# Gates of one dense tile scattered to memory as words, and 28 low parts of weights moved from GpSimd to VectorE

## Chip, cores and metric

One core of one Trainium2 chip. The metric is the device time of one execution in microseconds; lower is better. The kernel before took 2700.61 us (median of 3 runs, 2696.91 to 2716.93).

## What is computed

An encoder block: norm, a pooling and windowed-attention mixer with its output projection, norm, and an expert layer (PEER). The change touches the expert layer alone:

```python
def chunk(ht):                                   # 128 tokens
    q = (ht @ w_q).reshape(128, 8, 2, 128)       # 8 heads, 2 halves
    s = einsum('thpc,hpnc->thpn', q, subkeys)
    sv, si = top_k(s, 16)                        # 16 of 128 keys, each half
    cand_s = sv[:, :, 0, :, None] + sv[:, :, 1, None, :]
    cand_i = si[:, :, 0, :, None] * 128 + si[:, :, 1, None, :]
    top_s, top_pos = top_k(cand_s, 16)           # 16 experts a head
    expert = take_along_axis(cand_i, top_pos)
    gate = softmax(top_s)
    act = gelu(einsum('thkd,td->thk', u[expert], ht))
    return einsum('thkd->td', (gate * act) * v[expert])
```

There are 16384 experts (128 x 128), 1024 tokens of width 1024, so each token uses 8 x 16 = 128 gates.

## The kernel before

The 1024 tokens are 8 tiles of 128. Tiles 5 to 7 are "gathered": for each of their 128 gates a row of `u` and a row of `v` is fetched per token by an indirect DMA (GpSimd) and used on VectorE. Tiles 0 to 4 are "dense": every expert is computed for them on TensorE, and a full table of gates (zero where an expert isn't chosen) multiplies the result. Weights are multiplied in two parts, high and low: ScalarE rounds the raw piece `w_raw` to `w_hi` (`upper_ahead`, L961), and GpSimd makes `w_lo = w_raw - w_hi` (`lower_u`, L681). An item of the first dense stage is one 512 KB piece of `u` (or of the query weights, 16 of the 144 items) against 640 tokens: 48 matmuls of 320 columns (L1644), then Gelu (L955) and a store to `act_d` in HBM by SyncE.

The items fall into three stretches, which the text calls A, B and C:

- A, bodies 0 to 41 (2 items a body): the queries' items among them, while VectorE finds the best keys and pairs (`best_pairs`, `pair_keys`) and dots gathered `u` rows (`dot_row`, L1382). ScalarE takes the exponent of all gates at body 39; VectorE then divides by the sums (L1484 to L1486), and TensorE turns keys and gates (L1972) so that experts lie along partitions.
- B, bodies 42 to 61: 20 "strips" of 32 tokens. For four tokens at a time (`m`), VectorE writes one-hot tiles `is_i` and `gate_j` (L1508, L1512; ScalarE makes the fourth `gate_j`), TensorE multiplies them into a 128 x 128 gate table per token (`gates`, L1984, 4 times between the matmuls of each item), ScalarE copies it out (L989), and each strip of 2 MB goes to `g_d` in HBM. VectorE also dots 4 rows an item, GpSimd fetches 4 rows an item and makes one low part, which it starts after the item's first `gate_j` (a wait on `gj_done`).
- C, bodies 62 to 71: 20 items without gates. GpSimd makes one low part an item and fetches 3 or 4 rows, the last 40 of them `v` rows (L697), which VectorE adds with a scalar-tensor-tensor (`early_row`, L1397). ScalarE issues the first loads of stage 2 (`fetch`).

Each engine has its own program in a fixed order, and semaphores tie them. `w_raw`, `w_hi` and `w_lo` have two slots each: the load of a piece waits for the low part two items earlier, `w_hi` for TensorE's release of the slot, and TensorE waits for the low part. A row buffer is one of 8 (`RING`); in C the fetches run 6 rows ahead of the rows that VectorE has to have used by then.

Stage 2 reads `act_d` and the gates back (four dense tiles by `g_raw`, the fifth by `g_first`, 512 KB in runs of 1 KB), multiplies them (L1538, L1544), splits into high and low parts and multiplies with `v` (L2013), while GpSimd fetches the other `v` rows (L740) and VectorE adds them (L1588).

## Time and profile before

| quantity | us |
|---|---|
| median of 3 runs | 2700.61 |
| all runs | 2700.61, 2716.93, 2696.91 |
| profiled execution: span from first to last instruction | 2706.7 |
| TensorE busy (share of the span) | 2604.8 (96%) |
| VectorE busy | 2139.0 (79%) |
| GpSimd busy | 1490.1 (55%) |
| ScalarE busy | 881.3 (33%) |

The three runs have no record of what of them lies outside a span; the profiled execution's span is itself 6.1 us above the median of the three runs and inside their extent. A matmul's rows show pipelined instructions, so their distance in time is what one costs, not their length; an fp32 matmul appears as two rows.

### The profile page before, as it was taken

The numbers are of one execution on the slowest core, as the hardware profiler recorded it, in microseconds if no ns is written. First come the engines' busy times: TensorE is split into PE (matmuls) and PEld (weight loads), VectorE is DVE, ScalarE is ACT, GpSimd is POOL, SyncE is SP. The second block draws the span as 40 slices with busy tenths as digits, with TensorE's granted clock in tenths as the row PEclk, the third lists the DMA queues.
The fourth block names the chain that finished last, engine by engine and source line by source line (L and its number), as shares of the span: only waits on it lengthen the run. The fifth ranks groups of instructions, "written<-read, shape, count | busy, mean of one in ns | idle before, by whom it ended". The sixth has DMA issues, their size and how long they took to land.

```text
span 2706.7 us, 41554 instructions
## 1 busy us (share of the span) xinstructions
PE 2604.8 (96%) x15177; PEld 2334.8 (86%) x15177; DVE 2139.0 (79%) x4586; ACT 881.3 (33%) x1655; POOL 1490.1 (55%) x960
## 2 busy tenths in 40 slices
PE   7999989999999999989999999998999999999998
PEld 6777758999999999989999999986888787888887
DVE  6022273589888999999999995768998988998996
ACT  4223252222222222236666662222222222222222
POOL 1111020245666677766565557837777766776670
PEclk9999989999999999999999999998999999999999
DMA  4110013335777899989999999999999999999993
GB/s 147 47 32 24 24 56 125 107 108 164 278 273 257 306 317 318 338 307 354 389 373 377 379 394 348 406 341 366 388 388 388 353 384 370 386 385 388 384 382 128
DMA packets 296525, 763.31 MB, mean 282 GB/s; under 512 B 25808, under 2 KB 116304, under 8 KB 293584
## 3 DMA queue, kind: packets, MB, share of 16 engines
q0 software_dynamic: 110592, 402.70, 39.8%
q1 hardware_dynamic: 161280, 288.88, 30.8%
q10 hardware_dynamic: 24528, 70.26, 6.7%
q8 instruction: 54, 0.88, 0.1%
q14 instruction: 71, 0.58, 0.1%
HBM read 669.47 MB, written 92.27 MB: 281 GB/s over the span
## 4 chain that ended last, share of the span: by engine, by line
PE 63%; DVE 10%; DMA 6%; issue 4%; POOL 3%; ACT 1%; SPq 0%; DVEq 0%; ACTq 0%
PE bank L1644 27%; PE bank L2013 13%; PE wide L2013 10%; PE bank L1984 5%; DMA g_raw<-g_d 4%; PE bank L1893 3%; PE bank L1912 2%; DVE u_row L1382 1%; POOL w_lo L681 1%; DVE eq L1452 1%; DVE v_lo L1595 1%; POOL u_row L697 1%; PE bank L1921 1%; DMA u_row<-in_v,ids 1%; DVE route L1454 1%
## 5 line engine op out<-in xcount | busy, mean ns | idle before, releaser
L740 POOL DMA_INDIRECT d_row<-in_v,ids x344 | 591.7, 1720 | 276.6 <-DVE yg L1588 196.6
L1644 PE MATMUL bank<-h_hi,w_hi 128*128 128x320 f32 (+1 forms) x2368 | 562.3, 319 | 13.2 <-POOL w_lo L681 10.2
L1644 PE MATMUL bank<-h_hi,w_lo 128*128 128x320 f32 (+1 forms) x2368 | 545.7, 312 | 0.0
L1644 PE MATMUL bank<-h_lo,w_hi 128*128 128x320 f32 (+1 forms) x2368 | 544.9, 311 | 0.0
L681 POOL TENSOR_TENSOR w_lo<-w_raw,w_hi 128x1024 fp32r<-128x1024 f32 x144 | 358.4, 2489 | 289.2 <-ACT w_hi L961 158.1
L1382 DVE CUSTOM_DVE_ANT_0 u_row<-wide,u_row 128x1024 f32<-128x1024 f32 x384 | 449.1, 1219 | 18.0 <-DMA u_row<-in_u_rows,ids 15.8
L692 POOL DMA_INDIRECT u_row<-in_u_rows,ids x384 | 388.0, 1010 | 115.8 <-issue 74.1
L1588 DVE SCALAR_TENSOR_TENSOR yg<-d_row,uh,yg 128x1024 f32<-128x1024 f32 x344 | 426.0, 1276 | 1.4
L1644 PEld LDWEIGHTS bank<-h_hi,w_hi 128*128 128x128 f32 x2368 | 392.5, 189 | 19.9 <-ACT act_st L955 8.4
L1644 PEld LDWEIGHTS bank<-h_lo,w_hi 128*128 128x128 f32 x2368 | 398.5, 188 | 2.5
L1644 PEld LDWEIGHTS bank<-h_hi,w_lo 128*128 128x128 f32 x2368 | 397.4, 188 | 2.5
L670 POOL TENSOR_TENSOR w_lo<-w_raw,w_hi 128x1024 fp32r<-128x1024 f32 x36 | 87.3, 2430 | 395.0 <-ACT w_hi L754 395.0
L1056 ACT ACTIVATE v_hi<-v_raw 128x1024 fp32r<-128x1024 f32 x128 | 135.3, 1060 | 452.4 <-PE bank L2013 315.3
L2013 PE MATMUL bank<-v_hi,a_hi 128*128 128x512 f32 x768 | 237.0, 390 | 4.0 <-DVE a_lo L1552 4.0
L2013 PE MATMUL bank<-v_lo,a_hi 128*128 128x512 f32 x768 | 237.3, 390 | 0.0
L2013 PE MATMUL bank<-v_hi,a_lo 128*128 128x512 f32 x768 | 236.8, 390 | 0.0
L1595 DVE TENSOR_TENSOR v_lo<-v_raw,v_hi 128x1024 fp32r<-128x1024 f32 x128 | 155.4, 1216 | 43.6 <-ACT v_hi L1056 43.5
L2013 PE MATMUL wide<-v_hi,a_hi 128*128 128x512 f32 x512 | 162.7, 400 | 23.8 <-DVE y L1572 11.7
L955 ACT ACTIVATE act_st<-bank 128x320 f32<-128x320 f32 x200 | 75.6, 429 | 329.4 <-PE bank L1644 329.4
L1210 DVE CUSTOM_DVE_ANT_0 sc<-bank,bias 128x192 f32<-128x192 f32 (+2 forms) x96 | 29.8, 346 | 190.6 <-PE bank L1767 190.6
L2013 PEld LDWEIGHTS bank<-v_hi,a_hi 128*128 128x128 f32 x768 | 144.3, 188 | 34.2 <-issue 4.2
L1984 PE MATMUL bank<-gate_j,is_i 128*128 128x128 f32 x1280 | 169.1, 275 | 2.6 <-issue 2.6
(232 smaller groups left out, 4300.6 us busy)
## 6 DMA issues: line engine op xcount, KB each, us to landing
w_raw<-in_u SPq DMA_DIRECT2D x128, 512.0 KB, 5.2
v_raw<-in_v ACTq DMA_DIRECT2D x126, 512.0 KB, 7.4
act_d<-act_st SPq DMA_DIRECT2D x128, 320.0 KB, 6.2
g_d<-g_st SPq DMA_DIRECT2D x20, 2048.0 KB, 9.8
a_raw<-act_d SPq DMA_DIRECT2D x154, 256.0 KB, 12.5
g_raw<-g_d SPq DMA_DIRECT2D x120, 256.0 KB, 12.4
w_raw<-in_w_q SPq DMA_DIRECT2D x32, 512.0 KB, 3.7
w_raw<-in_w_in SPq DMA_DIRECT2D x20, 512.0 KB, 3.6
```

Source lines behind the costliest of these rows:

```text
L670: nc.gpsimd.tensor_tensor(dst, w_raw[:, n % 2, :], hi, ALU.subtract).then_inc(lo_done, 1)
L681: nc.gpsimd.tensor_tensor(w_lo[:, s % 2, :], w_raw[:, s % 2, :], w_hi[:, s % 2, :], ALU.subtract).then_inc(lo_done, 1)
L692: nc.gpsimd.indirect_dma_start(u_row[k % RING][:, :], None, u_rows, bass.IndirectOffsetOnAxis(ids[:, r:r + 1], 0)).then_inc(row_in[k % RIN ...
L740: nc.gpsimd.indirect_dma_start(d_row[k % DR][:, :], None, v_rows, bass.IndirectOffsetOnAxis(ids[:, c:c + 1], 0)).then_inc(d_in[k % DR], 16)
L1056: nc.scalar.activation(v_hi[:, j, :], v_raw[:, n % VR, :], ACT.Copy).then_inc(vh_done, 1)
L1382: V.tensor_tensor_reduce(u_row[n % RING][:, :], wide[:, :], u_row[n % RING][:, :], 1.0, 0.0, ALU.mult, ALU.add, uh[:, k:k + 1]).then_inc(r ...
L1588: V.scalar_tensor_tensor(out=yg[t][:, :], in0=d_row[k % DR][:, :], scalar=uh[:, c:c + 1], in1=yg[t][:, :], op0=ALU.mult, op1=ALU.add).then ...
L1595: V.tensor_tensor(v_lo[:, j, :], v_raw[:, n % VR, :], v_hi[:, j, :], ALU.subtract).then_inc(vl_done, 1)
L1644: ins = pe.matmul(banks[h][:, 0:n], lhs[:, part], rhs[:, k, h * n:(h + 1) * n], start=(k == 0 and lhs is lhs_hi and rhs is h_hi), stop=(k ...
L1893: ins = pe.matmul(bank[(2 * i + h) % 4 if i else 6 + h][:, :], lhs[:, k, toks], wo[k][:, rhs, h * HALF:(h + 1) * HALF], start=(k == 0 and ...
L1984: ins = pe.matmul(bank[4 + n % 2][:, k * NK:(k + 1) * NK], is_i[n % 4][:, k, :], gate_j[n % 4][:, k, :], start=True, stop=True)
L2013: ins = pe.matmul(bank[b + c][:, :], lhs[:, slot, c0:c0 + P], rhs[:, j, c * HALF:(c + 1) * HALF], start=start and lhs is a_hi and rhs is v ...
```

## The change

The last dense tile (tile 4, `SCAT`) gets its gates another way. Its 128 tokens leave the strips: 16 strips instead of 20, so B is bodies 42 to 57 and C is bodies 58 to 71 (28 items instead of 20). For this tile:

- early in the kernel SyncE writes zeros over an 8 MB table `g4_d` in HBM, 16 DMAs of 512 KB, two after each of eight pieces of the input projection;
- it is the first dense tile that VectorE works on; its gates are finished after the second, VectorE computes the word's place in the table for each gate (`gate_cells`), and ScalarE's exponent comes in two parts, at bodies 26 and 39;
- GpSimd issues 128 indirect DMAs, each of which writes 128 words (one gate of each token); the first 16 are plain writes, the others add. Two are issued an item in B (64 in all) and up to three an item in C (64 in 24 items), and before each group of 16 GpSimd waits until all earlier ones have landed;
- stage 2 loads `g_first` from this table in runs of 4 KB.

In C the low parts are made by VectorE (28 of them), ahead of each item's 3 or 4 rows, and GpSimd only waits for the item's high part to keep its pace.

```diff
-STRIPS = DS // TW
+SCAT = DT - 1
+RT = (SCAT // 2, SCAT // 2)
+STRIPS = SCAT * P // TW
...
+EXP_BODY_S = 26
+DENSE_ORDER = (SCAT, *range(SCAT))
+STRIP_SCAT = 2
+C_SCAT = 3
+ZERO_STEPS = 8
...
-            queue.dma_start(g_first[:, :, :], g_d[UNIT // TW:STRIPS, :, GT * g:GT * g + GT, :]
-                            .rearrange("b p j t -> p b (j t)")).then_inc(gf_in, 16)
+            queue.dma_start(g_first[:, :, :], g4_d[g]).then_inc(gf_in, 16)
...
+                if 8 <= n < 8 + ZERO_STEPS:
+                    if n == 8:
+                        sp.wait_ge(zero_set, 1)
+                    per = NG // ZERO_STEPS
+                    for g in range(per * (n - 8), per * (n - 7)):
+                        sp.dma_start(g4_d[g].rearrange("p (a j) t -> p a (j t)", j=2),
+                                     zeros[:, :].unsqueeze(1).broadcast_to([P, GT // 2, 2 * P])).then_inc(zero_out, 16)
...
+            def scatter_gates(count):
+                for k in range(scattered[0], min(scattered[0] + count, P)):
+                    if k == 0:
+                        pool.wait_ge(zero_out, 16 * NG)
+                        pool.wait_ge(cell_done, 1)
+                    elif k % TOP == 0:
+                        pool.wait_ge(cell_out, 16 * k)
+                    nc.gpsimd.indirect_dma_start(g4_cells, bass.IndirectOffsetOnAxis(cell[:, k:k + 1], 0),
+                                                 route[:, 2, SCAT, k:k + 1], None,
+                                                 compute_op=ALU.add if k >= TOP else ALU.bypass
+                                                 ).then_inc(cell_out, 16)
+                    scattered[0] = k + 1
+                    if (k + 1) % TOP == 0:
+                        break
...
                 lower_u(B0 + n // 2, n % 2)
                 gathers_u(ROWS_FRONT + RING + ROW_AT[n + 1])
+                scatter_gates(STRIP_SCAT)
             for n in range(2 * (ITEM_BODIES - C0)):
-                lower_u(C0 + n // 2, n % 2)
+                pool.wait_ge(hi_done, W_U0 + 2 * C0 + n + 1)
                 gathers_u(ROWS_C + RING - 2 + (n + 1) * ROWS_BODY_C // 2)
+                scatter_gates(C_SCAT)
...
+            act.wait_ge(g_ask, NGT + 1)
+            nc.scalar.activation(route[:, 2, SCAT:NT, :], route[:, 2, SCAT:NT, :], ACT.Exp).then_inc(g_e, 1)
...
+                    act.wait_ge(cell_out, 16 * P)
                     load_first(act, 0)
...
+            def gate_cells():
+                one, two = route[:, 0, SCAT, :], route[:, 1, SCAT, :]
+                a, b = idf[:, 0:P], idf[:, P:2 * P]
+                group([gates_of(SCAT, NT, 1),
+                       V.tensor_copy(cell[:, :], two),
+                       V.scalar_tensor_tensor(out=a, in0=one, scalar=float(GT), in1=two, op0=ALU.mult, op1=ALU.add)])
...
+            def lower_u(t):
+                dve.wait_ge(hi_done, W_U0 + t + 1)
+                V.tensor_tensor(w_lo[:, t % 2, :], w_raw[:, t % 2, :], w_hi[:, t % 2, :],
+                                ALU.subtract).then_inc(lo_last, 1)
...
+            for n in range(2 * (ITEM_BODIES - C0)):
+                lower_u(2 * C0 + n)
+                while used[0] < min(ROWS_C + (n + 1) * ROWS_BODY_C // 2, ROW_ITEMS):
+                    dot_row()
...
-                pe.wait_ge(lo_done, it * 2 + (W_U0 + s + 1))
+                if last:
+                    pe.wait_ge(lo_last, it * 2 + (s + 1 - 2 * C0))
+                else:
+                    pe.wait_ge(lo_done, it * 2 + (W_U0 + s + 1))
```

GpSimd's program in stretch B, before: an item is one low part and four fetches of rows (`ids` holds the experts' numbers).

```order
L681 TENSOR_TENSOR w_lo<-w_raw,w_hi 128x1024
L692 DMA u_row_127<-in_u_rows,ids 128x1024
L692 DMA u_row_128<-in_u_rows,ids 128x1024
L692 DMA u_row_121<-in_u_rows,ids 128x1024
L692 DMA u_row_122<-in_u_rows,ids 128x1024
L681 TENSOR_TENSOR w_lo<-w_raw,w_hi 128x1024
```

The same place in the changed program; `cell` holds the words' places, `route` the gates.

```order
L709 TENSOR_TENSOR w_lo<-w_raw,w_hi 128x1024
L720 DMA u_row_130<-in_u_rows,ids 128x1024
L720 DMA u_row_131<-in_u_rows,ids 128x1024
L720 DMA u_row_124<-in_u_rows,ids 128x1024
L720 DMA u_row_125<-in_u_rows,ids 128x1024
L754 DMA g_d<-route,cell 2097152x1 x2
L709 TENSOR_TENSOR w_lo<-w_raw,w_hi 128x1024
```

Two indirect DMAs of words follow the four fetches of each item, ahead of the next item's low part.

VectorE's program where B ends and C begins, before (`uh` holds the dot products, then gates times activations):

```order
L1508 TENSOR_TENSOR is_i_134<-iota,route_t 128x512
L1512 TENSOR_SCALAR gate_j_138<-iota,route_t 128x128 x3
L1382 ISA u_row_127,uh<-wide,u_row_127 128x1024
L1382 ISA uh 128x1
L1403 TENSOR_TENSOR uh<-uh,gate_g 128x256
L1397 SCALAR_TENSOR_TENSOR yg_166<-u_row_128,uh,yg_166 128x1024
L1382 ISA u_row_121,uh<-wide,u_row_121 128x1024
L1382 ISA uh 128x1
L1397 SCALAR_TENSOR_TENSOR yg_167<-u_row_122,uh,yg_167 128x1024
L1397 SCALAR_TENSOR_TENSOR yg_166<-u_row_123,uh,yg_166 128x1024
```

The same place in the changed program:

```order
L1591 TENSOR_SCALAR gate_j_141<-iota,route_t 128x128 x3
L1598 TENSOR_TENSOR w_lo<-w_raw,w_hi 128x1024
L1442 ISA u_row_130,uh<-wide,u_row_130 128x1024
L1442 ISA uh 128x1
L1442 ISA u_row_131,uh<-wide,u_row_131 128x1024
L1442 ISA uh 128x1
L1463 TENSOR_TENSOR uh<-uh,gate_g 128x256
L1457 SCALAR_TENSOR_TENSOR yg_169<-u_row_124,uh,yg_169 128x1024
L1598 TENSOR_TENSOR w_lo<-w_raw,w_hi 128x1024
L1442 ISA u_row_125,uh<-wide,u_row_125 128x1024
L1442 ISA uh 128x1
L1457 SCALAR_TENSOR_TENSOR yg_170<-u_row_126,uh,yg_170 128x1024
```

Each low part stands ahead of an item's rows, and behind all rows of the item before, each of which waits for its fetch.

## Rows read from the trace of the kernel before

**Rows 1.** The page, part 4: the chain that ended last, by engine.

```profile
PE 63%; DVE 10%; DMA 6%; issue 4%; POOL 3%; ACT 1%; SPq 0%; DVEq 0%; ACTq 0%
```

**Rows 2.** Windows in B (first two) and C (last): busy us, clock, DMA share, GB/s.

```profile
1316.00:1422.00 106.00, 106.00 (x804) 106.00 (x803) 102.81 (x243) 70.11 (x150) 62.36 (x51) 1.00 0.98 377
1528.00:1634.00 106.00, 106.00 (x804) 106.00 (x803) 95.38 (x227) 67.75 (x144) 60.50 (x49) 1.00 0.99 390
1686.00:1736.00 50.00, 47.71 (x320) 46.73 (x319) 34.29 (x30) 11.66 (x21) 44.18 (x30) 1.00 1.03 409
```

**Rows 3.** Timeline, ScalarE: ends of items in A, B, and first and last of C.

```profile
1155.31 0.77 ACT L955 ACTIVATE act_st<-bank 128x320 f32<-128x320 f32 x2 [5.33 <-PE bank L1644]
1162.35 0.77 ACT L955 ACTIVATE act_st<-bank 128x320 f32<-128x320 f32 x2 [1.66 <-PE bank L1644]
...
1297.04 0.74 ACT L955 ACTIVATE act_st<-bank 128x320 f32<-128x320 f32 x2
...
1307.62 0.74 ACT L955 ACTIVATE act_st<-bank 128x320 f32<-128x320 f32 x2
...
1635.28 0.77 ACT L955 ACTIVATE act_st<-bank 128x320 f32<-128x320 f32 x2 [0.19 <-PE bank L1644]
...
1786.21 0.77 ACT L955 ACTIVATE act_st<-bank 128x320 f32<-128x320 f32 x2 [6.28 <-PE bank L1644]
```

**Rows 4.** Timeline, GpSimd: one item of B and the start of the next.

```profile
1310.50 2.40 POOL L681 TENSOR_TENSOR w_lo<-w_raw,w_hi 128x1024 fp32r<-128x1024 f32 x1 [3.31 <-DVE gate_j L1512]
1313.04 0.95 POOL L692 DMA_INDIRECT u_row<-in_u_rows,ids  x1
1314.29 0.94 POOL L692 DMA_INDIRECT u_row<-in_u_rows,ids  x1 [0.30 <-issue]
...
1321.08 2.39 POOL L681 TENSOR_TENSOR w_lo<-w_raw,w_hi 128x1024 fp32r<-128x1024 f32 x1 [3.31 <-DVE gate_j L1512]
```

**Rows 5.** Groups by line, GpSimd in C: its fetches.

```profile
L697 POOL DMA_INDIRECT u_row<-in_v,ids x35 | 40.2, 1149 | 10.8 <-issue 8.1 <-DVE yg L1397 1.9 <-DVE uh L1382 0.6
L692 POOL DMA_INDIRECT u_row<-in_u_rows,ids x22 | 29.3, 1332 | 5.8 <-issue 4.9 <-DVE uh L1382 0.9
```

**Rows 6.** Timeline in C: a fetch on GpSimd, and VectorE at that time.

```profile
1669.58 1.59 POOL L692 DMA_INDIRECT u_row<-in_u_rows,ids  x1 [0.31 <-issue]
...
1669.07 2.54 DVE L1397 SCALAR_TENSOR_TENSOR yg<-u_row,uh,yg 128x1024 f32<-128x1024 f32 x2
```

**Rows 7.** Waits in C.

```profile
DVE yg L1397 <- DMA u_row<-in_v,ids: 33.9, 23, 6.5
PE bank L1644 <- POOL w_lo L681: 5.7, 8, 1.4
```

**Rows 8.** DMA issues: out<-in, queue, count, KB each, median us to landing.

```profile
g_first<-g_d SPq DMA_DIRECT2D x15, 512.0 KB, 18.3
x_d<-xs SPq DMA_DIRECT2D x8, 512.0 KB, 2.6
u_row<-in_v,ids POOLq DMA_INDIRECT x40, 12.8
```

**Rows 9.** Groups by line, VectorE: a low part of stage 2.

```profile
L1595 DVE TENSOR_TENSOR v_lo<-v_raw,v_hi 128x1024 fp32r<-128x1024 f32 x128 | 155.4, 1216 | 43.6 <-ACT v_hi L1056 43.5
```

**Rows 10.** DMA queues in 1316:1528 (first row) and in 2300:2500 (other rows).

```profile
q1 hardware_dynamic: 7221, 38.07, 45.7%
...
q1 hardware_dynamic: 25039, 18.80, 30.0%
q10 hardware_dynamic: 4366, 15.87, 20.1%
```

**Rows 11.** Timeline, VectorE where A ends: the gates' sums and division.

```profile
1191.31 1.22 DVE L1484 TENSOR_REDUCE gsum<-route 128x64 f32<-128x1024 f32 x1
1193.15 2.64 DVE L1486 TENSOR_TENSOR route<-route,gsum 128x1024 f32<-128x1024 f32 x1
```

**Rows 12.** Window in the first projections: busy us, clock, DMA share, GB/s.

```profile
100.00:300.00 200.00, 192.26 (x997) 144.18 (x995) 39.65 (x171) 57.33 (x156) 26.06 (x11) 0.98 0.11 32
```

More of the change, by code:

```diff
@@ L55 @@
 C0 = B0 + STRIPS
+W_C0 = W_U0 + 2 * C0
 ROWS_EARLY = 4
@@ L315, in build @@
         g_raw = [at(f"g_raw{s}", base, [P, UNIT // TW, VJ * TW]) for s, base in enumerate((198, 70))]
-        g_first = at("g_first", 78, [P, P // TW, GT * TW])
+        g_first = at("g_first", 78, [P, GT, P])
         a_hi = at("a_hi", 96, [P, RA, UNIT], F32R)
@@ L383, in build @@
         g_ask = sem("g_ask")
+        lo_last = sem("lo_last")
+        row_set = sem("row_set")
+        zero_set = sem("zero_set")
+        zero_out = sem("zero_out")
+        cell_done = sem("cell_done")
+        cell_out = sem("cell_out")
         route_done = sem("route_done")
@@ L524, in load_piece @@
             def load_piece(n, src):
-                if n >= 2:
+                if n - 2 >= W_C0:
+                    sp.wait_ge(lo_last, n - 1 - W_C0)
+                elif n >= 2:
                     sp.wait_ge(lo_done, n - 1)
@@ L972, in _ @@
                 upper_ahead(0, t)
-            with act.Fori(BODY1, EXP_BODY) as it:
+            with act.Fori(BODY1, EXP_BODY_S) as it:
+                for s in range(2):
+                    chunk(it, s)
+            act.wait_ge(g_ask, NGT + 1)
+            nc.scalar.activation(route[:, 2, SCAT:NT, :], route[:, 2, SCAT:NT, :], ACT.Exp).then_inc(g_e, 1)
+            with act.Fori(EXP_BODY_S, EXP_BODY) as it:
                 for s in range(2):
@@ L1170, in _ @@
             dve.wait_ge(cst_in, 16 * 6)
+            V.tensor_tensor_reduce(pb_[:, 0:P], ident[:, :], iota[:, :], 1.0, 0.0, ALU.mult, ALU.add,
+                                   row_no[:, 0:1]).then_inc(row_set, 1)
+            dve.wait_ge(row_set, 1)
             for c in range(2):
@@ L1473, in _, with gates_of @@
             assert used[0] == ROWS_Q
-            for t in range(DT):
+            def gates_of(t0, t1, exps):
+                dve.wait_ge(g_e, exps)
+                gate = route[:, 2, t0:t1, :].rearrange("p t (h k) -> p t h k", h=PH)
+                group([V.tensor_reduce(gsum[:, 0, t0:t1, :], gate, AX.X, ALU.add)])
+                group([V.reciprocal(gsum[:, 1, t0:t1, :], gsum[:, 0, t0:t1, :])])
+                return V.tensor_tensor(gate, gate, gsum[:, 1, t0:t1, :].unsqueeze(3)
+                                       .broadcast_to([P, t1 - t0, PH, TOP]), ALU.mult)
+            def gate_cells():
[4 more added lines that the diff above has]
+                       V.scalar_tensor_tensor(out=a, in0=one, scalar=float(GT), in1=two, op0=ALU.mult, op1=ALU.add)])
+                group([V.tensor_scalar(cell[:, :], cell[:, :], NK - GT, None, ALU.bitwise_and),
+                       V.tensor_scalar(a, a, float(P), row_no[:, 0:1], ALU.mult, ALU.add),
+                       V.tensor_copy(gate_g[:, :, :], route[:, 2, DT:NT, :])])
+                group([V.tensor_copy(b, cell[:, :])])
+                group([V.scalar_tensor_tensor(out=a, in0=b, scalar=float(P * P - P), in1=a, op0=ALU.mult, op1=ALU.add)])
+                V.tensor_copy(cell[:, :], a).then_inc(cell_done, 1)
+            for n, t in enumerate(DENSE_ORDER):
                 best_pairs(t, ROWS_TILE // 4)
@@ L1478, in _ @@
                 pair_keys(t, ROWS_TILE // 4)
-                for r in range(ROWS_TILE // 2 - ROWS_TILE // 4 if t + 1 < DT else 0):
+                if n == 1:
+                    gate_cells()
+                for r in range(ROWS_TILE // 2 - ROWS_TILE // 4 if n + 1 < DT else 0):
                     dot_row()
-            dve.wait_ge(g_e, 1)
-            gate = route[:, 2, :, :].rearrange("p t (h k) -> p t h k", h=PH)
-            group([V.tensor_reduce(gsum[:, 0, :, :], gate, AX.X, ALU.add)])
-            group([V.reciprocal(gsum[:, 1, :, :], gsum[:, 0, :, :])])
-            V.tensor_tensor(gate, gate, gsum[:, 1, :, :].unsqueeze(3).broadcast_to([P, NT, PH, TOP]),
-                            ALU.mult).then_inc(route_done, 1)
+            gates_of(0, SCAT, 2).then_inc(route_done, 1)
             while used[0] < ROWS_FRONT:
                 dot_row()
-            dve.wait_ge(route_done, 1)
-            group([V.tensor_copy(gate_g[:, :, :], route[:, 2, DT:NT, :])])
             for n in range(6):
                 dve.wait_ge(rt_done, n + 1)
-                V.tensor_copy(route_t[:, n // 2, n % 2 * TT[0] * P:n % 2 * TT[0] * P + half_width(n)],
+                V.tensor_copy(route_t[:, n // 2, n % 2 * RT[0] * P:n % 2 * RT[0] * P + half_width(n)],
                               bank[4 + n % 2][:, 0:half_width(n)]).then_inc(rt_ev, 1)
@@ L1943, in _, with chunk @@
                 gathered_scores(hp)
-            def chunk(it, s, first, between=None):
-                pe.wait_ge(lo_done, it * 2 + (W_U0 + s + 1))
+            def chunk(it, s, first, between=None, last=False):
+                if last:
+                    pe.wait_ge(lo_last, it * 2 + (s + 1 - 2 * C0))
+                else:
+                    pe.wait_ge(lo_done, it * 2 + (W_U0 + s + 1))
                 if first:
@@ L1970, in _ @@
                     pe.wait_ge(rt_ev, n - 1)
-                for q in range(TT[n % 2]):
-                    ins = pe.transpose(bank[4 + n % 2][:, q * P:(q + 1) * P], route[:, n // 2, TT[0] * (n % 2) + q, :],
+                for q in range(RT[n % 2]):
+                    ins = pe.transpose(bank[4 + n % 2][:, q * P:(q + 1) * P], route[:, n // 2, RT[0] * (n % 2) + q, :],
                                        ident[:, :])
@@ L2003, in _ @@
                 for s in range(2):
-                    chunk(it, s, False)
+                    chunk(it, s, False, last=True)
             PARTS = ((a_hi, v_hi), (a_hi, v_lo), (a_lo, v_hi))
```

26 lines of the change are left out of this document (17 added, 9 removed).

## Prediction

> **What bounds the kernel now.** I read the page's chain first: TensorE carries 63% of it, VectorE 10% and the DMAs 6% [rows 1], so the change is worth what it takes out between TensorE's matmuls, if nothing else becomes late. Next the table of windows over stretches B and C [rows 2]. In B TensorE is busy all of the time, at the full clock, but so are VectorE (102.81 of 106 us) and the 16 DMA engines (share 0.98 to 0.99). In C's middle TensorE lacks 5%, VectorE has room, GpSimd is busy 44.18 of 50 us, and the DMAs are at 1.03. So four resources stand within a few per cent of the end; that is what the prediction turns on. Then ScalarE's timeline, whose Gelu follows each item's end [rows 3]: an item takes 1162.35 - 1155.31 = 7.04 us in A, 1307.62 - 1297.04 = 10.58 us in B, and in C the last of 20 ends 1786.21 - 1635.28 = 150.9 us after the last of B, 7.55 us each. The matmuls of an item are the same in all three, so its gates cost 10.58 - 7.04 = 3.54 us, and C loses 0.51 us an item to something else.
>
> What that is the engines' timelines tell. GpSimd in B [rows 4]: 2.40 us for the low part, 0.14 us of gap, then four fetches 1.25 us from start to start, 7.5 us in all; then it waits 3.31 us for VectorE's `gate_j`, which only sets its pace. In C it has no such room: the fetches take 40.2 + 29.3 = 69.5 us for 57, 1.22 us each instead of 0.95, with 13.0 us of "issue" between [rows 5]. That is 1.45 us each from start to start. The long ones lie beside VectorE's additions of rows: a fetch of 1.59 us stands beside two of them [rows 6]. The waits of C say the rest: TensorE waited 5.7 us in 8 places for GpSimd's low part, and VectorE 33.9 us for rows to land [rows 7]. The Trainium skill (SBUF — State Buffer, Who interferes with whom) says that a VectorE instruction with two SBUF inputs contends with a GpSimd instruction that reads SBUF; the trace agrees with it in C.
>
> **The change, part by part.** *Fewer strips.* Eight items go from B to C. B becomes 32 x 10.58 = 338.6 us, 84.6 us less.
>
> *C with 28 items.* With TensorE as the only bound these items take 28 x 7.04 = 197.1 us, 46.2 us more than the 150.9 us now, and the change would save 38.4 us. I don't expect that, for GpSimd. It loses the low parts but gets 64 scatters. Its DMAs in C: 424 row items in all, less the 326 that VectorE has used by then, less the 8 that were fetched ahead, make 90; with 64 scatters 154. At B's 1.25 us each they need 192 us, at C's 1.45 us 223 us. I take 1.45 us: VectorE's additions stay, and its low parts, again with two SBUF inputs, come to them, while the low part on GpSimd, behind which a fetch was often late, goes. Rows that come late hold VectorE, and in its new order the low part of the next item stands behind all rows of the item before, so TensorE waits in turn. The head start of 6 rows, and the last four items without scatters, give some of it back; the four waits for a whole group of 16 to land take some (a fetch lands after 12.8 us in the median in C's kind, and the words stand behind fetches [rows 8]). I let these cancel. C: 223 us, 72.1 us more than now. VectorE itself has the time: a low part 1.22 us [rows 9] and 3.5 rows of some 1.2 us are 5.4 of 7.04 us.
>
> The DMA engines' bound on C lies beside it. Its bytes: 90 rows, 26 loads of `u` and 28 stores of 320 KB (47.2 + 13.6 + 9.2 MB), the last strip 2.1 MB, and the first loads of stage 2, about 7.3 MB, 79.4 MB together. At that window's 409 GB/s [rows 2] that is 194 us without the words.
>
> *Two scatters an item in B.* GpSimd's item grows from 7.5 us by 2 x 1.25 us to 10.0 us, below 10.58 us, if a scatter costs it what a fetch does; no row shows a scatter. From below it is 0.94 us (nothing less than a fetch's own time), from above the slow fetch of rows 6, 1.59 us and 0.3 us of gap, 1.9 us. I take 1.25 to 1.45 us. Then B keeps its pace; for the four waits on landed groups and for crowded DMAs I add 3 us.
>
> *The words as DMA work.* 128 DMAs bring 8 words to each of 16 engines. What a small packet takes comes from two windows of q1 [rows 10]: 0.300 x 16 x 200 us over 25039 packets is 38 ns for 751 bytes, 0.457 x 16 x 212 us over 7221 is 215 ns for 5272 bytes. The line through both has 9 ns without any byte. That is the lower bound; the upper one is q10's 0.201 x 16 x 200 / 4366 = 147 ns for a packet of 3.6 KB. An adding word is read and written, so I take some 25 ns: 16 words an item in B are 0.4 us of an engine's 10.58 us, twice what the share of 0.98 leaves, which the 3 us cover. In C 64 x 8 x 25 ns = 13 us on 194 us stay below 223 us. At 147 ns it would be 2.35 us an item in B and 75 us in C.
>
> *Zeros.* Sixteen stores of 512 KB go out among SyncE's first projections. A store of that size lands after 2.6 us [rows 8], two are 5 us ahead of a piece's load, eight times. The DMA share there is 0.11, and TensorE is busy 192.26 of 200 us [rows 12]. Each piece is loaded well ahead, so 0 us; without that cover up to 8 x 5 = 42 us.
>
> *Where A ends.* VectorE is the last there: it sums and divides the gates of eight tiles, 1.22 and 2.64 us among it [rows 11]. Half of that is now done earlier, but so are nine small steps for the words' places, and all of it is on VectorE, which had no room in A. I take +4 us earlier, -2.5 us here (half of those two and a copy that moves with them): +1.5 us. ScalarE's second exponent has 5.33 us of idle time to hide in [rows 3].
>
> *`g_first` in runs of 4 KB.* By the line above 512 packets of 1 KB cost 16 engines 1.57 us, 128 of 4 KB 1.35 us. This load took 18.3 us to land [rows 8], and stage 2 is full; -2 us, between 0 and -10 us.
>
> *Sum.* -84.6 + 72.1 + 3 + 0 + 1.5 - 2 = -10 us. The profiled execution's span of 2706.7 us becomes 2696.7 us; the median of the runs lies 6.1 us below that span, so the forecast is 2690.6 us, 0.4% less. A measurement of this kernel can tell about 1%, 27 us, from no change.
>
> **Rivals.** *TensorE alone bounds C.* If GpSimd's fetches fall back to 1.25 us because its own low parts were what slowed them, 192 us of DMAs fit beside 197 us. For it: in B fetches are 0.95 us long beside one-hots [rows 4]. Against it: rows 6. Time: 2700.6 - 38.4 + 1.5 - 2 = 2662 us.
>
> *A scatter costs GpSimd much more than a fetch* (slower). Place: GpSimd's item in B, where the next low part stands behind the two scatters. It decides from 1.5 us a scatter: 7.5 + 3.0 is B's 10.58 us. At the upper bound of 1.9 us B's item is 11.3 us, 0.72 x 32 = +23 us, and C is 90 x 1.45 + 64 x 1.9 = 252 us, +29 us on my 223: 2690 + 52 = 2742 us. With waits of the groups on top it ends near 2760 us. For it: 112 of them add, which no row shows. Against: a fetch makes 128 transfers too, in 0.94 us.
>
> *The words clog the DMA engines* (slower). At 80 ns a word B's item gets 1.28 us of engine time against 0.2 us of room, 1.1 x 32 = +35 us, C 194 + 41 = 235 us, +12 us; less the 3 us already counted, 2734 us. For it: share 0.98 [rows 2]. Against: 9 ns on the line of rows 10. The Trainium skill (DMA: Bandwidth & Descriptors, Specifications) says that below 512 bytes the DMA engine does a read-modify-write; by that rule this rival is the likelier one, and no run here shows a word's price.
>
> **How the numbers follow.** The forecast is the likeliest, 2690.6 us. Forecast 0.43, TensorE-bound 0.20, slow scatters 0.20, slow words 0.14, something else 0.03. The forecast's own range is 2672 to 2706 us. Faster by over 1%: all of the second and a sixth of the first, 0.27. Slower by over 1%: three quarters of the two slow ones, 0.26. Within 1%: 0.47. The range of 8 in 10 reaches from 2655 us to 2762 us.
>
> **What would show it.** B's items stay at 10.58 us and TensorE stays full there; GpSimd is busy in nearly all of B. C's items take about 8 us, with VectorE waiting for rows and TensorE for `w_lo` from VectorE. GpSimd's word DMAs last 0.95 to 1.2 us. The forecast is wrong if an item in B is over 10.8 us, if C's items are at 7.04 us, or if the word DMAs last over 1.5 us.

## The result and the profile after

The changed kernel takes 2779.1 us (median of 4 runs, 2773.1 to 2782.2), the kernel before 2701.2 us (4 runs). The ratio on record is 1.0263, with a 95% interval of 1.0229 to 1.0298; the two medians alone give 1.029. It is slower, by 2.6% or a little more. The forecast was 2690.6 us with a range up to 2762 us, so both missed.

The three ends of the stages come from ScalarE's timeline of the changed kernel: first and last item of B, the item before which ScalarE stops, and the last item of C. The columns are start, duration, engine and line, what it writes and reads, and in brackets the idle time before it and its releaser.

```profile
1224.88 0.74 ACT L1004 ACTIVATE act_st<-bank 128x320 f32<-128x320 f32 x2
...
1581.13 0.77 ACT L1004 ACTIVATE act_st<-bank 128x320 f32<-128x320 f32 x2 [0.20 <-PE bank L1732]
...
1806.88 0.44 ACT L1004 ACTIVATE act_st<-bank 128x320 f32<-128x320 f32 x1 [10.28 <-issue]
...
1832.30 0.44 ACT L1004 ACTIVATE act_st<-bank 128x320 f32<-128x320 f32 x1 [23.70 <-DMA g_d<-route,cell]
...
1859.56 0.77 ACT L1004 ACTIVATE act_st<-bank 128x320 f32<-128x320 f32 x2 [6.81 <-PE bank L1732]
```

These answer to [rows 3]. B's 31 items from the first end to the last take 356.3 us, 11.5 us each; 10.58 was forecast. C takes 1859.6 - 1581.1 = 278.4 us; 223 was forecast, and its 20 items took 150.9 us before. Near its end ScalarE stands still for 23.7 us, until the last word has landed, before it may load `g_first`. Stage 2 is as it was: 2779.5 - 1859.6 = 919.9 us against 2706.7 - 1786.2 = 920.5 us. So the 72.8 us between the two spans arise in B and C, but for 2 us in A, whose end moved from 1222.9 to 1224.9 us: B is 56 us shorter where 85 were forecast (356.3 us from its first end to its last against 412.4 before), and C is 127.5 us longer where 72 were forecast.

The windows of the same stretches as [rows 2], and last the first projections of [rows 12], in the changed kernel (busy us of TensorE, its weight loads, VectorE, ScalarE and GpSimd, clock, DMA share, GB/s):

```profile
1316.00:1422.00 106.00, 99.80 (x739) 97.56 (x738) 105.82 (x229) 64.66 (x139) 90.81 (x64) 1.00 0.93 338
1686.00:1736.00 50.00, 35.75 (x225) 34.45 (x224) 25.44 (x31) 8.54 (x15) 39.58 (x29) 0.95 0.94 292
100.00:300.00 200.00, 192.07 (x995) 144.14 (x991) 39.29 (x166) 56.49 (x153) 26.82 (x12) 0.98 0.22 69
```

In B TensorE is no longer full (99.80 of 106 us), and the DMA engines carry less than before (share 0.93 for 0.98, 338 GB/s for 377). DMA engines that clog B would be at a share near 1. In C's window TensorE is busy 71% of the time; the DMA share is 0.94, but with 292 GB/s for 409, so there the share alone decides nothing (the runs below do). The zeros of the table show only as DMA share and GB/s in the last row; TensorE's 192.07 us are the 192.26 of [rows 12].

GpSimd's groups by line, first in B (1212:1570; what follows the bar is busy us and mean ns of one, then idle us before them and its releasers), then in C (1570:1860):

```profile
L754 POOL DMA_INDIRECT g_d<-route,cell x62 | 91.2, 1471 | 18.9 <-issue 18.9
L709 POOL TENSOR_TENSOR w_lo<-w_raw,w_hi 128x1024 fp32r<-128x1024 f32 x31 | 86.7, 2796 | 9.2 <-DVE gate_j L1591 8.7
...
L754 POOL DMA_INDIRECT g_d<-route,cell x66 | 117.3, 1777 | 27.1 <-issue 18.9 <-DMA g_d<-route,cell 7.3 <-DVE yg L1457 0.9
L720 POOL DMA_INDIRECT u_row<-in_u_rows,ids x55 | 57.2, 1041 | 16.8 <-issue 16.2 <-DVE yg L1457 0.3 <-DVE uh L1442 0.3
L725 POOL DMA_INDIRECT u_row<-in_v,ids x39 | 40.3, 1032 | 13.1 <-issue 10.5 <-ACT w_hi L1010 1.7 <-DVE uh L1442 0.9
```

Here the word DMAs (L754) stand out: 1.47 us in B, with the 16 plain ones among them, and 1.78 us in C. The forecast took the duration of a fetch. GpSimd's wait for VectorE's `gate_j`, 3.31 us an item in [rows 4], is down to 8.7 us over the whole of B. In the second window its 160 DMAs, six of them of B's last item, are busy 214.8 us and idle 57.0 us before them, mostly the 0.3 us between any two ("issue"). That makes 271.8 us, beside 278.4 us for C: it is the engine that paces C. A fetch costs 97.5 / 94 + 29.9 / 94 = 1.36 us from start to start, a word 117.3 / 66 + 27.1 / 66 = 2.19 us.

The waits of C in the changed kernel, answering to [rows 7] (us in total, times, longest):

```profile
DVE u_row L1442 <- DMA u_row<-in_u_rows,ids: 73.6, 21, 6.1
PE bank L1732 <- DVE w_lo L1598: 50.1, 17, 6.7
DVE yg L1457 <- DMA u_row<-in_v,ids: 40.7, 18, 5.7
ACT act_st L1004 <- DMA g_d<-route,cell: 23.7, 1, 23.7
```

This is the chain the forecast described, with larger numbers: GpSimd asks for rows late, VectorE waits 114 us for them, and its low part, in order behind them, is late for TensorE by 50.1 us.

### The profile page after: what moved, and what is told of

It reads as the page before. It is cut to its first block, busy times and chain, and to the rows that moved or that the text cites. A ratio compares the mean times of both kernels' runs of the same rounds, so it can differ in the third digit from the quotient of the medians.

```text
span 2779.5 us, 40906 instructions
## 1 busy us (share of the span) xinstructions
PE 2603.8 (94%) x14918; PEld 2323.5 (84%) x14918; DVE 2145.2 (77%) x4499; ACT 856.2 (31%) x1574; POOL 1632.1 (59%) x1060
## 3 DMA queue, kind: packets, MB, share of 16 engines
q0 software_dynamic: 127232, 402.78, 40.4%
## 4 chain that ended last, share of the span: by engine, by line
PE 40%; DVE 21%; POOL 9%; issue 9%; DMA 5%; ACT 2%; another core or an unknown queue 1%; SPq 0%; DVEq 0%; ACTq 0%; POOLq 0%
PE bank L2104 13%; PE wide L2104 9%; PE bank L1732 9%; DVE u_row L1442 6%; POOL g_d L754 4%; DMA g_raw<-g_d 4%; POOL u_row L720 3%; PE bank L1981 2%; PE bank L2075 2%; PE bank L2000 2%; POOL w_lo L709 1%; DVE eq L1512 1%; DVE eq L1510 1%; DVE route L1514 1%; DVE rest_k L1409 1%
## 5 line engine op out<-in xcount | busy, mean ns | idle before, releaser
L1732 PE MATMUL bank<-h_hi,w_hi 128*128 128x320 f32 (+1 forms) x2368 | 571.1, 323 | 84.0 <-DVE w_lo L1598 50.1
L1732 PE MATMUL bank<-h_lo,w_hi 128*128 128x320 f32 (+1 forms) x2368 | 552.3, 315 | 1.1 <-issue 1.1
L1732 PE MATMUL bank<-h_hi,w_lo 128*128 128x320 f32 (+1 forms) x2368 | 551.9, 315 | 0.0
L1732 PEld LDWEIGHTS bank<-h_hi,w_hi 128*128 128x128 f32 x2368 | 398.7, 192 | 99.3 <-issue 48.5
L720 POOL DMA_INDIRECT u_row<-in_u_rows,ids x384 | 397.5, 1035 | 121.4 <-issue 81.7
L1732 PEld LDWEIGHTS bank<-h_lo,w_hi 128*128 128x128 f32 x2368 | 405.4, 191 | 4.6 <-issue 2.0
L1732 PEld LDWEIGHTS bank<-h_hi,w_lo 128*128 128x128 f32 x2368 | 404.2, 191 | 2.6
L709 POOL TENSOR_TENSOR w_lo<-w_raw,w_hi 128x1024 fp32r<-128x1024 f32 x116 | 303.8, 2620 | 154.8 <-ACT w_hi L1010 138.2
L698 POOL TENSOR_TENSOR w_lo<-w_raw,w_hi 128x1024 fp32r<-128x1024 f32 x36 | 87.4, 2431 | 394.4 <-ACT w_hi L803 394.4
L754 POOL DMA_INDIRECT g_d<-route,cell x128 | 208.5, 1629 | 46.0 <-issue 37.8
```

The source lines that it names most:

```text
L698: nc.gpsimd.tensor_tensor(dst, w_raw[:, n % 2, :], hi, ALU.subtract).then_inc(lo_done, 1)
L709: nc.gpsimd.tensor_tensor(w_lo[:, s % 2, :], w_raw[:, s % 2, :], w_hi[:, s % 2, :], ALU.subtract).then_inc(lo_done, 1)
L720: nc.gpsimd.indirect_dma_start(u_row[k % RING][:, :], None, u_rows, bass.IndirectOffsetOnAxis(ids[:, r:r + 1], 0)).then_inc(row_in[k % RIN ...
L754: nc.gpsimd.indirect_dma_start(g4_cells, bass.IndirectOffsetOnAxis(cell[:, k:k + 1], 0), route[:, 2, SCAT, k:k + 1], None, compute_op=ALU. ...
L1732: ins = pe.matmul(banks[h][:, 0:n], lhs[:, part], rhs[:, k, h * n:(h + 1) * n], start=(k == 0 and lhs is lhs_hi and rhs is h_hi), stop=(k ...
```

## The experiments

Theory 1: an adding word takes GpSimd's own time, far more than a fetch, and GpSimd paces B and C. Rivals: the words' packets clog the DMA engines; VectorE's low parts cost C its pace; waits for landed words do it. Each ratio is against the kernel before on the same chip, with its 95% interval.

**All words plain.**

```diff
-                                                 compute_op=ALU.add if k >= TOP else ALU.bypass
+                                                 compute_op=ALU.bypass
```

> The changed kernel with all 128 word DMAs as plain writes, none adds (gates of an expert that two heads of a token share are not summed). Theory 1, GpSimd's time for an adding DMA: a word DMA falls from 1.6 to about 1.05 us on GpSimd, an item of B from 11.5 to 10.6 to 10.8 us, C from 278 to about 212 us, in all about 2690 us (2670 to 2710). Theory 2, the words' work in the DMA engines: as many packets are left, so over 2755 us. Theory 3, VectorE's low parts in C: nothing changes, 2770 to 2785 us.

2709.6 us, ratio 1.0023 (1.0008 to 1.0039): at the upper end of what was expected, with C at 237.9 us for 212. The same 128 DMAs write the same words, and nearly all of the loss is gone. It is not the same number of packets, though. GpSimd's queue on the pages of the changed kernel, of this one and of the kernel before:

```profile
q0 software_dynamic: 127232, 402.78, 40.4%
```

```profile
q0 software_dynamic: 114688, 402.78, 40.0%
```

```profile
q0 software_dynamic: 110592, 402.70, 39.8%
```

A plain DMA of words makes (114688 - 110592) / 128 = 32 packets, an adding one (127232 - 110592 - 16 x 32) / 112 = 144. So the expectation that "as many packets are left" was wrong, and this run alone does not part GpSimd's time from the work of the packets; a pair on one chip does so below.

**No words.** `scatter_gates` only counts, so the last dense tile's gates stay zero, and ScalarE doesn't wait for words.

```diff
             def scatter_gates(count):
+                scattered[0] = P
+                return
...
-                    act.wait_ge(cell_out, 16 * P)
```

> The changed kernel without the 128 word DMAs (the fifth dense tile gets zeros for gates). It shows all that the words cost, by any way. Theory 1: B at 10.6 us an item, C at 7.1 us, about 2668 us. Theory 2 expects the same here. Theory 3: C stays long, over 2740 us.

2672.2 us, ratio 0.987 (0.985 to 0.989). B stays at 10.6 us an item, and C takes 1754.8 - 1548.2 = 206.6 us by ScalarE's timeline, near the 197 us of TensorE alone. Without the words the rest of the change would gain 1.3%; even plain ones cost some 37 us.

**Low parts alone.** The kernel before, with the 20 low parts of its C on VectorE, each ahead of the rows of its item.

```diff
-                lower_u(C0 + n // 2, n % 2)
+                pool.wait_ge(hi_done, W_U0 + 2 * C0 + n + 1)
...
+            for n in range(2 * (ITEM_BODIES - C0)):
+                lower_u(2 * C0 + n)
+                while used[0] < min(ROWS_C + (n + 1) * ROWS_BODY_C // 2, ROW_ITEMS):
+                    dot_row()
```

> The kernel before with one part of the change alone: VectorE makes the low parts of the 20 items of C, all gates stay with the strips. Theory 1: GpSimd gets free room, an item of C falls from 7.55 to about 7.1 us, 8 us less than before: about 2692 us. Theory 3: the low parts behind the rows on VectorE hold TensorE, C is longer than before, 2705 us or more.

2704.4 us, ratio 1.000 (0.9986 to 1.0014): the 8 us didn't come. C takes 148.6 us for 150.9 before. Its first items ran at 7.04 us, but four of the last eight took 7.6 to 12.0 us. VectorE's timeline near C's end reads

```profile
1754.19 1.22 DVE L1523 TENSOR_TENSOR w_lo<-w_raw,w_hi 128x1024 fp32r<-128x1024 f32 x1
...
1760.81 1.28 DVE L1401 SCALAR_TENSOR_TENSOR yg<-u_row,uh,yg 128x1024 f32<-128x1024 f32 x1 [1.13 <-DMA u_row<-in_v,ids]
1764.19 1.29 DVE L1401 SCALAR_TENSOR_TENSOR yg<-u_row,uh,yg 128x1024 f32<-128x1024 f32 x1 [2.10 <-DMA u_row<-in_v,ids]
1765.39 1.22 DVE L1523 TENSOR_TENSOR w_lo<-w_raw,w_hi 128x1024 fp32r<-128x1024 f32 x1
```

Two low parts are 11.2 us apart, because the rows between them land late (5.0 us of waits for four rows). That is the price of a low part in order behind rows: TensorE's faster pace is given back when the rows don't keep up.

**Low parts back on GpSimd**, in the changed kernel.

```diff
-                pool.wait_ge(hi_done, W_U0 + 2 * C0 + n + 1)
+                lower_u(C0 + n // 2, n % 2)
```

> The changed kernel with the 28 low parts of C back on GpSimd. Theory 1: GpSimd bounds C and gets 28 x 2.4 = 67 us more, so about 2840 us (2820 to 2860). Theory 3: under 2779 us.

2826.9 us, ratio 1.0446 (1.0428 to 1.0464). In the changed kernel the low parts on VectorE are worth 48 us (2826.9 - 2779.1), or 58 us against the 2768.7 us that it takes on another chip (below). The rival that blamed them falls.

**Words first in an item of B.**

```diff
-                gathers_u(ROWS_FRONT + RING + ROW_AT[n + 1])
                 scatter_gates(STRIP_SCAT)
+                gathers_u(ROWS_FRONT + RING + ROW_AT[n + 1])
```

> The changed kernel with one order changed in stage B: in each item GpSimd issues its two words behind the low part and ahead of the four fetches, not behind them. In the changed kernel the low part that follows two adding words lasts 2.97 us, and 2.40 without adds. Theory 1a (an adding word leaves work behind on GpSimd that lengthens whatever comes next): the low part goes back to 2.40 us, the first fetch behind the words lengthens by about 0.5 us, and the item stays at 11.7: 2779. Theory 1b (the low part is slowed by something else in the stage, such as VectorE's port or the adds' traffic in SBUF): the low part stays near 2.9 us and the fetches at 1.05; again 2779. If an item falls under 11.2 us, an ordering effect that neither names is there: under 2768.

2771.7 us, ratio 1.0242 (1.0212 to 1.0272), as theory 1a said. Its low parts last 2.39 us, the first fetch behind the words 1.30 us for 0.97, and from one low part's start to the next it is 11.7 us still. VectorE's compare overlaps this low part too, which is no longer for that, so VectorE doesn't explain the longer one of the changed kernel.

**The load of `g_first` behind ScalarE's last item**; the other loads of gates move ahead of it. In one run with adding words, and in one with plain ones.

```diff
                 elif n == AR + G_PARTS:
-                    act.wait_ge(cell_out, 16 * P)
-                    load_first(act, 0)
+                    load_g(act, 0, 1, 0)
...
+            act.wait_ge(cell_out, 16 * P)
+            load_first(act, 0)
             act.wait_ge(row_used, ROW_ITEMS)
```

> The changed kernel with one transfer moved: the load of the fifth tile's first gates (g_first), which waits on ScalarE for all 128 word DMAs and stood 23.7 us at the sixth last item of the last stage before the row reductions end, now stands behind ScalarE's last item; the other four gate loads move ahead of it. Theory 1 (GpSimd's own time, not ScalarE's wait, bounds the last stage): GpSimd has the same 94 fetches and 66 words to issue, so the stage keeps most of its 278 us; the items behind the wait run at up to 9 to 10 us instead of 5.5, so at most 15 us go: 2765 to 2779. Rival (the wait is an extra stop that nothing overlaps): the whole 23.7 us go: 2755. If g_first now arrives too late for stage 2, up to 5 us come back at its start.

2770.8 us, ratio 1.0247 (1.023 to 1.0265), 8 us below the first runs of the changed kernel, which were not taken beside it. ScalarE's 23.7 us are not the loss: GpSimd still has all its DMAs to issue.

> Plain words throughout (gates of experts shared by heads are not summed) and the load of the fifth tile's first gates behind ScalarE's last item. With plain words alone the kernel took 2709.6 us and ScalarE waited 19.8 us for the words, with stage C at 238 us. Theory 1 (GpSimd's issue time bounds C, 94 fetches at 1.34 us and 66 words at 1.4 to 1.5 give 220 to 225 us, and the wait for the last word adds to it): C 222 to 232 us, 2694 to 2704. Rival (the wait in ScalarE is hidden, GpSimd has no slack): 2710. Rival (the wait is the whole loss of plain words against none): C near 215, 2688.

2755.7 us, ratio 1.0175 (1.0156 to 1.0194): 46 us over the highest of the three expectations, and B at 11.3 us an item with plain words, which had run at 10.6 in the first run of plain words.

**Half of the words plain** (`ALU.add if k >= P // 2`).

> The changed kernel with words 0 to 63 written plainly (so gates of experts shared by heads are not summed there) and words 64 to 127 still added. Words 0 to 61 belong to the one-hot stage B, the others to the last stage C. Theory 1 (an adding word costs GpSimd about 0.6 us more than a plain one, in the item in which it stands): B at 10.6 us an item (339 us, as with plain words throughout), C as in the changed kernel, 278 us: 2779 - 28 = 2750. Rival (the adds' cost is a delayed one, through waits at C's end for the whole chain of words): B as now, at 11.5 us, or C shorter than 260.

2764.2 us, ratio 1.0206 (1.0189 to 1.0224), and again B at 11.3 us with plain words: its 31 items take 351.1 us, 5 us less than the changed kernel's 356.3, where 28 were expected. Both last runs were taken on another chip than the first four. The waits of TensorE from 1200 to 1920 us with plain words and the late load on that chip, and of the same kernel on the third one:

```profile
PE bank L1733 <- issue: 41.5, 67, 1.5
PE bank L2076 <- issue: 8.2, 17, 1.5
```

```profile
PE bank L1733 <- DVE w_lo L1599: 25.1, 13, 3.8
...
PE bank L2076 <- issue: 1.1, 1, 1.1
```

On one chip TensorE waited 49.7 us for nothing that the trace names, inside items, 84 times; on the other 1.1 us. So the next four went to one chip together. The stalls are no constant of the second chip either: the run with the words first had 7.8 us of them there, the changed kernel with the late load 10.6 us, the half-plain one 18.2 us.

> The kernel of e1_plain once more (128 plain words, ScalarE's wait for them where the change put it, gates of shared experts not summed). In e1_plain its one-hot stage ran at 10.6 us an item and TensorE had no unexplained stall there; e8_plain_late and e6_half_plain, with the same plain words in that stage, ran at 11.3 us an item with 10 to 12 us of stalls of TensorE that the trace puts down to issue, and e1_plain and these were taken on two chips. Theory P (the stalls belong to the program): 2702 to 2722 again, no stalls. Theory C (the stalls belong to the chip or to where a run's memory lies): here it takes either, and e12_plain_late_again beside it takes the same kind.

> The kernel of e8_plain_late once more, beside e9_plain_again on one chip. Theory P (the stalls of TensorE at issue belong to the program): 2748 to 2757 again, with some 50 us of such stalls. Theory C (they belong to the chip or the placing of memory): without them 2694 to 2704, as first expected of e8_plain_late.

2710.1 us for plain words again, ratio 1.0023 (1.0012 to 1.0035), and 2705.4 us with the late load, 1.0004 (0.9988 to 1.002). Theory P falls: the stalls don't belong to the program, for the same program ran 50 us faster here. The half-plain run can't be read for the split between B and C, and with plain words the late load is worth some 5 us, which the two intervals barely tell from nothing.

> The changed kernel itself once more, beside the plain-word kernels on one chip. Both theories expect 2773 to 2785; what it adds is the cost of adding against plain words on one chip: by theory 1 of the first runs 65 to 75 us between this and e9_plain_again, if neither has stalls at issue beyond the 13 us seen in the changed kernel.

2768.7 us, ratio 1.024 (1.0215 to 1.0264), 58.7 us over plain words beside it, where 65 to 75 were expected. It is also 4 us under the expected 2773 to 2785, which rest on the first runs: TensorE's unexplained waits, 13.4 us in the changed kernel's first profile, are 1.3 us here. This pair gives the split. By ScalarE's timelines B's 31 items take 1571.60 - 1222.58 = 349.0 us against 1546.09 - 1218.43 = 327.7 us (+21.3), C takes 1852.35 - 1571.60 = 280.8 against 1786.86 - 1546.09 = 240.8 us (+40.0); the rest of the 65.3 us between these two spans is A's end.

GpSimd's words in C, first with adding words (1571:1852), then with plain ones (1546:1790):

```profile
L754 POOL DMA_INDIRECT g_d<-route,cell x64 | 118.2, 1846 | 24.5 <-issue 18.3 <-DMA g_d<-route,cell 5.9 <-DVE yg L1457 0.3
```

```profile
L754 POOL DMA_INDIRECT g_d<-route,cell x64 | 72.0, 1125 | 24.3 <-issue 18.0 <-DMA g_d<-route,cell 5.4 <-DVE uh L1442 0.9
```

With the idle time before it, an adding word costs (118.2 + 24.5) / 64 = 2.23 us here and a plain one 1.50 us. The 64 words make 46 us more, and the fetches beside them 1.36 us each for 1.48, some 10 us less; together 37 of the 40 us. This pair also settles the packets. GpSimd waited 5.9 us for landed words with adds and 5.4 us without. The fetches of `u` rows landed after 5.8 us in the median in C with adds, after 6.8 us without: the DMA engines didn't deliver later. Two things did change there without setting the pace. The packets of GpSimd's queue took 0.570 x 280.8 = 160.1 us of the 16 engines' time for 0.542 x 240.8 = 130.5 us. And TensorE's granted clock over C was 0.88 for 0.96, its busy time 228.3 us for 209.2 us for as many matmuls; GpSimd waited only 2.0 us for ScalarE's `w_hi`, so this slower TensorE hardly held it.

GpSimd in B of this run, first an item with plain words, then one with adding words:

```profile
1249.19 2.40 POOL L709 TENSOR_TENSOR w_lo<-w_raw,w_hi 128x1024 fp32r<-128x1024 f32 x1
1251.75 0.98 POOL L720 DMA_INDIRECT u_row<-in_u_rows,ids  x1 [0.16 <-issue]
...
1256.89 1.00 POOL L754 DMA_INDIRECT g_d<-route,cell  x1 [0.30 <-issue]
1258.20 1.05 POOL L754 DMA_INDIRECT g_d<-route,cell  x1 [0.30 <-issue]
1259.26 2.41 POOL L709 TENSOR_TENSOR w_lo<-w_raw,w_hi 128x1024 fp32r<-128x1024 f32 x1
```

```profile
1452.30 2.95 POOL L709 TENSOR_TENSOR w_lo<-w_raw,w_hi 128x1024 fp32r<-128x1024 f32 x1
1455.42 1.27 POOL L720 DMA_INDIRECT u_row<-in_u_rows,ids  x1 [0.17 <-issue]
...
1461.06 1.62 POOL L754 DMA_INDIRECT g_d<-route,cell  x1 [0.31 <-issue]
1462.99 1.59 POOL L754 DMA_INDIRECT g_d<-route,cell  x1 [0.30 <-issue]
1464.03 2.96 POOL L709 TENSOR_TENSOR w_lo<-w_raw,w_hi 128x1024 fp32r<-128x1024 f32 x1
```

The plain item takes 1259.26 - 1249.19 = 10.07 us, the 10.0 us of the forecast. The adding one takes 1464.03 - 1452.30 = 11.73 us, over TensorE's 10.58 us, and then GpSimd sets B's pace. Two adding words cost 1.66 us more than two plain ones: 0.62 us between the two words' starts (1.93 for 1.31), 0.56 us in the low part, and 0.50 us over the four fetches (5.64 us from the first fetch to the first word, for 5.14). The low part's record begins 0.55 us before the second word's ends, so its 0.56 us may be the end of that word rather than a slower low part.

**One word an item in B**, 32 there and 96 in C.

```diff
-STRIP_SCAT = 2
-C_SCAT = 3
+STRIP_SCAT = 1
+C_SCAT = 4
```

> The changed kernel with one word an item in the one-hot stage B and up to four in C (32 and 96 instead of 62 and 66): work moved, none removed. Theory 1 (GpSimd's own time): B's item needs 2.4 to 2.7 + 4 x 1.35 + 1.9 = 10.0 us of GpSimd, so B goes back to TensorE's 10.6 us and wins 29 us; C gets 30 more adding words at 1.9 to 2.1 us, 57 to 63 us, so 335 to 340 us against 278: 2804 to 2812. Rival (a word costs little in C because GpSimd waits there anyway): C within 300, under 2775. The best number of words per item would then be fewer in B.

2798.2 us, ratio 1.0349 (1.0324 to 1.0373). B's items are at 10.6 us throughout, and C is 49 us longer than in the changed kernel on that chip, for 30 more words: 1.6 us each. Work was moved to where GpSimd has less room.

**22 words at the end of A**, one an item from item 62 on, with the two constants of the run before.

```diff
                     gathers_u(rows_by(t) + 5)
+                if t >= SCAT_ITEM:
+                    scatter_gates(1)
```

> The kernel of e11_one_each (one word an item in B, up to four an item in C) with 22 words, one an item, issued at the end of stage A, from its item 62 on; C has 74 words instead of 96. Theory 1 (a word costs GpSimd's own time where that bounds the pace): C loses 22 adding words at 2.0 us, 44 us; A, where GpSimd waits 25 us in its last 23 items (1.1 us an item), takes 16 plain words at 1.3 and 6 adding ones at 1.9 us, so 5 to 10 us come back: 2798 - 44 + 8 = 2762, 2755 to 2772. Rival (the word itself costs, wherever it stands): 2790 to 2800.

2776.5 us, ratio 1.0258 (1.022 to 1.0296), on a fourth chip. Against one word an item, A is 8 us longer (first item of B ends at 1234.3 for 1226.5), as expected (16 of its words are plain); C is 35 us shorter for 22 words less, 1.6 us each where 2.0 was expected. The time came between the two expectations, 4 us above the range of theory 1. A word is cheap where GpSimd waits and dear where it doesn't. The rival of a price that follows the word, with 2790 to 2800 us, falls: 22 words more made A 8 us longer, and 22 fewer made C 35 us shorter.

**Words placed by GpSimd's spare time**: 22 in A, one and two in turn in B (`scatter_gates(1 + n % 2)`), the rest in C, and the late load.

> All 128 words placed by GpSimd's spare time: 22 in A (one an item from item 62 on), one and two in turn in B's items (some 48), 58 in C at up to three an item, and the load of the first gates behind ScalarE's last item. Against the changed kernel by theory 1: B back to 10.6 us an item, -21; C with 58 words for 66, -16; A +8; the load moved, -5: 2769 - 34 = 2735, 2718 to 2750: better than the change, and not better than the kernel before (2705), which would need words of under 1.0 us. Rival (the word itself costs, wherever it stands): 2760 to 2770.

2757.0 us, ratio 1.0191 (1.015 to 1.0232), the best of the placements that add, but 22 us over the expectation and 7 us over its range. Its C is 259 us, 21 us shorter than the changed kernel's 281. B shows why less came of it: GpSimd now meets the wait for a group of 16 in the middle of an item, one item behind the words it waits for.

```profile
1304.52 1.61 POOL L755 DMA_INDIRECT g_d<-route,cell  x1 [3.62 <-DMA g_d<-route,cell]
...
1310.51 0.90 PE L1736 MATMUL bank<-h_hi,w_hi 128*128 128x320 f32 x2 [3.23 <-POOL w_lo L710]
```

GpSimd waits 3.62 us for words to land, its low part is late, and TensorE waits 3.23 us for it; the item takes 15.6 us. This happens again at the end of B, with 4.3 us.

No version that writes all gates beats the kernel before. The low parts alone take as long as it does, and plain words (2705 to 2710 us) come near, but they don't sum the gates of shared experts.

## Why the prediction was wrong

**The step that failed** is the one under *Two scatters an item in B*: "I take 1.25 to 1.45 us" for a scatter, by what a fetch costs. For a plain word this holds: 1.31 us from start to start in B, and the item at 10.07 us. An adding word costs 0.83 us more there (1.66 / 2), 2.1 us. No row of before showed an adding DMA, so the value taken had to stand between bounds; the upper bound of 1.9 us, from the slowest fetch, was itself too low. The decision point was given rightly: over 1.5 us a scatter B's item passes 10.58 us. B came out at 11.5 x 32 = 368 us instead of 338.6 + 3. Some of this is not the words: on the third chip, without the stalls, it is 349.0 / 31 x 32 = 360 us, with the items of the 16 plain words still at 10.58 us.

**The same price in C.** The forecast had 154 DMAs at 1.45 us, 223 us. There were 160 (66 words and 94 fetches): the fetches cost 94 x 1.36 = 128 us, near the 130 us forecast for 90, the words 66 x 2.19 = 144 us instead of 64 x 1.45 = 93. These 51 us are nearly all of the 55 us by which C missed. ScalarE's 23.7 us wait for the last word was not forecast. Its removal gained some 5 us with plain words (2710.1 - 2705.4) and 8 us with adding ones (2779.1 - 2770.8, not on one chip), since GpSimd bounds C with it or without.

**With plain words** the forecast's prices stand: 1.31 us a word in B, 1.50 us a word and 1.48 us a fetch in C, for 1.25 to 1.45 us taken. The time was 2710 us for 2691, above the forecast's own range (to 2706 us) and inside the wide one, with B at 10.6 us an item and C at 240.8 us for 223. The DMAs of that C sum to 64 x 1.50 + 89 x 1.48 = 228 us; the other 13 us the forecast's sum had no term for. So even with the price of a plain word the true answer was no change, and not 10 us less.

**Words as DMA work.** Right that it doesn't set the pace; the size is not confirmed. 25 ns a word were taken, against 147 ns as the upper bound. With plain words B ran at 10.6 us an item, at TensorE's pace. With adding ones GpSimd's queue took (160.1 - 130.5) / 64 = 0.46 us more of all 16 engines' time per DMA in C. That is 58 ns a word on top of a plain one, by 8 words an engine, an estimate that puts all of it on the words; in B's items of the same pair no difference shows. The 144 packets that an adding DMA makes were not foreseen. The Trainium skill (DMA: Bandwidth & Descriptors, Specifications) has a read-modify-write below 512 bytes. Whether it took place no trace here shows; if it did, it cost too little for plain words to slow an item of B.

**VectorE and GpSimd on one port.** The Trainium skill (SBUF — State Buffer, Who interferes with whom), named for C, describes B after the change too: there both instructions have two inputs. In the run of the changed kernel on the third chip, VectorE's first compare of a group, which begins beside GpSimd's low part, takes 2.33 us, its later ones 0.68 us:

```profile
1453.48 2.33 DVE L1587 TENSOR_TENSOR is_i<-iota,route_t 128x512 f32<-128x512 f32 x1
...
1456.51 0.68 DVE L1587 TENSOR_TENSOR is_i<-iota,route_t 128x512 f32<-128x512 f32 x1
```

The low part ends at 1455.25, and the compare 0.56 us later, about its own length. So VectorE's 105.82 of 106 busy us in the window above are partly a wait, and VectorE is not the bound there. The Trainium skill calls the shared port pair an exclusive lock there; these rows agree.

**The small terms.** Zeros at 0 us: right (TensorE's windows agree to 0.2 us). A's end at +1.5 us: the first item of B ends at 1224.9 us in the changed kernel's first profile and at 1222.6 in its second, for 1222.9 before. `g_first` at -2 us: stage 2 moved by 0.6 us, which can't be told from nothing.

**The rivals.** The one that came true is the slow scatter, given 0.20: its place (the low part behind the two scatters), its decision point and its sign were right, and its 2742 to 2760 us fell short of 2769 to 2779 because the bound was short. TensorE alone as C's bound (2662 us) did not come with words, adding or plain; only the kernel without words came near it, at 2672 us and 206.6 us for C. The rival of clogged engines fell. The low-part half of the change, forecast to give C room on GpSimd, does: 48 us. That it gives nothing in the kernel before was not foreseen.

**Left open.** Why an adding indirect DMA holds GpSimd longer, and slows the instructions behind it in B, no run here takes apart. Its 144 packets for 32 may be the reason, but no run varied them by themselves. What made TensorE stall without a named cause on the second chip is open too, as is how the stalls depend on the kernel; the kernel before took 2706.7 us there and 2704.9 us on the third, so it hardly suffers.

## What to carry to other kernels

Price a kind of instruction that the trace doesn't show from a run of that kind alone, if one can be had, before a schedule is built on it: here most of the loss hung on one duration that stood at 0.94 us for its nearest relative and at 1.6 us, with 0.2 us more in what follows, for itself. Where an engine has a fixed number of us to spare in each item, count what is moved onto it item by item against that room (3.1 us of GpSimd's in B held two plain words and not two adding ones), and look for the stage where it waits. Work that is moved ahead of or behind waits in one engine's order brings those waits to whoever needs it, as the low parts behind VectorE's rows show.
